# A reordered opening and a mixed gating and pooling stage in a two-branch encoder kernel on eight cores

## The chip, the cores and the metric

The kernel runs on one Trainium2 chip, on all 8 of its cores. Each core works on its own share of the data and no core talks to another. The time of a run is device microseconds of the slowest core. Five engines of a core matter here. PE (TensorE) multiplies matrices and writes to PSUM. DVE (VectorE), ACT (ScalarE) and POOL (GpSimd) do elementwise work. SP (SyncE) issues transfers only. ACT and POOL have DMA queues of their own as well. Each engine executes its own instructions in program order and waits on semaphores for the others.

## What is computed

One layer of a streaming encoder. Each row of x (1024 channels) is normalised and multiplied by `w_in`, which gives seven parts. They feed two branches, whose outputs are merged and projected back:

```python
h = _rmsnorm(x, norm_g)
a, g_a, u, v, g_b, r_a, r_b = jnp.split(h @ w_in, idx, axis=-1)   # 512 x5, 1024 x2
# A: per group of 128 channels, mean over a trailing window of 2/4/8/16 rows, minus a itself
pa = pool_mix(a, prev, pos0)
y_a = (silu(g_a) * (pa @ w_pool[g] * pool_scale)) @ w_a
# B: layer norm of v over its 512 channels, then rows mixed inside chunks of 128 positions
y_b = (silu(g_b) * (u * (W_s @ layernorm(v) + b_s))) @ w_b
y = x + (sigmoid(r_a) * y_a + sigmoid(r_b) * y_b) @ w_o
out = _rmsnorm(y, final_g)
```

There are 4 prompt streams of 8192 rows and 32 sample streams of 64 rows with a 15-row history for the pooling branch. A core gets half a prompt stream (4096 rows), 16 rows ahead of it (the halo, `xh`), and 4 sample streams (256 rows). Last rows of `a` and the normalised `v` of the sample rows are outputs too.

## The kernel before

The rows of a core are cut into eight prompt tiles of 512 rows and one sample tile of 256 rows. The sample tile is second. The first two tiles, t0 (prompt) and t1 (sample), are worked on together, since during them the weights are still arriving. From the third tile on each runs alone.

Weights come as blocks: `Win` is 18 blocks of 256 output columns, named by the part they belong to (C_V, C_GB, C_U, C_A, C_GA, C_RA, C_RB and +256), and `Wa`, `Wb` are four blocks each. All are cast from float32 to bfloat16 on the way, so they go through POOL's queue. `load_weights(n)` issues the next n blocks of a list, `order`. Each issue stands in POOL's program among small arithmetic (line 298 to 300, 1/sqrt of a mean; line 388, the mean of v), so it goes out only when POOL has reached it.

A tile passes these steps:

- x, 128 rows at a time ("sub-tile"): ACT squares and sums (`prep_square`, line 308), POOL makes 1/sqrt, DVE scales (`prep_scale`, line 317). In the opening PE transposes (line 332) and ACT copies the result to `hT` (line 336). Later tiles are transposed by DMA.
- v: PE multiplies (line 352, in the opening by halves of 256 columns, line 373). DVE takes statistics (lines 385 and 386), POOL makes scale and shift, and DVE (line 392) or ACT (line 395) normalises into `n`. For the sample tile ACT does this twice (line 399).
- stage B, four groups of 128 channels: PE makes g_b, ACT takes silu (line 478), PE makes u, DVE multiplies (line 483). One group later PE mixes positions (`z_group`, line 499), DVE adds the bias (line 512) and multiplies into `s` (line 515).
- stage A, four groups: PE makes a and g_a, ACT copies a (lines 430 or 426) and takes silu of g_a (line 434). Window sums are one to four doublings (line 443), on DVE for prompt tiles and on POOL for the sample tile. DVE subtracts (line 450), fixes the first 16 rows (lines 454, 456) and saves the last 16 (line 461). `a_finish` multiplies by `w_pool` on PE (the matmul with `Wp`) and DVE scales into `fa` (line 468).
- stage M, eight blocks: PE makes r_a and r_b, ACT takes sigmoids, PE multiplies `fa` by `Wa` and `s` by `Wb`, DVE merges (lines 531 to 537). Stage O: PE multiplies by `Wo` (line 544), DVE adds x, normalises and SP stores.

The order on every engine is the order in which the code calls these helpers. Nothing is rescheduled. `Sched` turns the named reads and writes of each call into semaphore waits. Three rings of buffers tie the engines to each other: 8 PSUM banks (`next_ps`), 10 work buffers in SBUF (`next_tmp`) and 5 buffers for x. A taker of a ring buffer waits for the last reader of what was there.

The opening is written out by hand (lines 669 to 795). Then stage B runs for t0 and t1 alternately, group by group, then stage A in the same way, then M of t0, M of t1, O of both. Matmuls that only spread a row over partitions (lines 687, 720, 636) come first on PE.

Of the kernel before, what the change touches and what calls it, by code (L numbers as in the profile page):

```python
# [12 lines left out]
P = 128  # L13
# [5 lines left out]
H = 16  # L19
# [105 lines left out]
def build_program(NT):  # L125
# [35 lines left out]
    with ExitStack() as st:  # L161
# [162 lines left out]

        def transpose_pe(xi, dst, kdst, n=P):
            bank, bk = next_ps()
            ptv = bfview(bank)

            def tr(e):
# [90 lines left out]
        def a_group(t, g):  # L420
# [52 lines left out]
        def gb_mm(t, g):  # L473
            return win_group(t, C_GB + g * P)
# [183 lines left out]
        def make_invc():  # L658
# [4 lines left out]
            for g, w in enumerate(WINDOWS):  # L663
# [38 lines left out]

        order = [C_GB, C_U, C_GB + 256, C_U + 256, C_A, C_GA, "Wp", C_A + 256, C_GA + 256]
        for i in range(4):
# [34 lines left out]

        def start_v(i, h=None):  # L740
            if i not in vb:
                vb[i] = next_ps()
            for hh in range(2) if h is None else (h,):
                v_half(*subs[i], hh, *vb[i])

        def start_stats(i):
            return v_stats(*subs[i], *vb[i], i < 4)

        early = {}
        cb = spread_bs()  # L750
        pk = start_square(0)
        xk[2] = load_x_sub(t0, 2, (), "act")
        xk[4] = load_x_sub(t1, 0, (), "act")
        S.add("act", lambda e: e.activation(out=identb[:, :], in_=identf[:, :], func=AF.Copy), ["identf"], ["identb"])
        c = start_xpose(0, prep_scale(pk))
        cb()
        for i in range(1, 4):
            xi = prep_scale(start_square(i))
            c()
# [36 lines left out]

# [34 lines left out]
        def stage_B(ts, pend, early=(), before_z=None):  # L831
# [159 lines left out]
```

How the kernel before makes its waits and increments, by code:

```python
    def emit_engine(self, eng_name, eng):  # L98
        seen = {}
        for op in self.ops[eng_name]:
            for d in op.deps:
                sem, val = d.token
                if seen.get(id(sem), 0) >= val:
                    continue
                seen[id(sem)] = val
                eng.wait_ge(sem, val)
            ins = op.emit(eng)
            if op.token is not None:
                if op.is_dma:
                    ins.then_inc(op.token[0], 16)
                else:
                    ins.then_inc(op.token[0], 1)
```

## Time and profile before

| what | value |
|---|---|
| median of 3 runs | 833.52 us (833.43 to 834.39) |
| the profiled execution's own time | 833.35 us |
| its span, first to last instruction | 831.8 us (cores 829.7 to 831.8) |
| PE busy | 801.5 us (96%) |
| DVE, ACT, POOL busy | 490.8 us (59%), 272.8 us (33%), 119.2 us (14%) |
| mean granted clock of TensorE, by core | 0.992 to 0.997 |
| first x transpose on PE | starts at 10.08 us |
| first matmul of stage B | starts at 42.76 us |
| first matmul with Wa (merging of t0) | starts at 95.84 us |

The page is of the slowest core. PE busy is the time that matmuls cover. They overlap, so the step from one start to the next is shorter than what one lasts. Idle time of PE is shown with what ended it. In the opening the engines wait for x and weights and for each other. From 100 us on PE hardly waits.

### The profile page before, as it was taken

The page shows a single profiled execution, that of the slowest core. Times are in us where ns is not written, and L with a number is a line of the kernel's source. Part 1 is how long each engine was busy: PE and PEld are TensorE (multiplying, and loading weights), DVE is VectorE, ACT ScalarE, POOL GpSimd, SP SyncE. Part 2 cuts the span into 40 slices and gives each one's busy share as a digit, 9 for nine tenths or more (in the row PEclk, how much of TensorE's full clock was granted, in tenths as well). Part 3 has the DMA queues.
Part 4 walks back from the last instruction along what each step waited for, and adds up shares of the span by engine and source line. Part 5 has one row for each costly group of instructions (what it writes and reads, how often), then busy time and mean ns, then how long its engine had stood idle before and what let it go on. Part 6 is the DMA issues. An engine that isn't in the chain of part 4 may idle for free.

```text
span 831.8 us, 13064 instructions; the slowest of 8 cores (829.7 to 831.8 us)
## 1 busy us (share of the span) xinstructions
PE 801.5 (96%) x4032; PEld 389.1 (47%) x4032; DVE 490.8 (59%) x801; ACT 272.8 (33%) x456; POOL 119.2 (14%) x296
## 2 busy tenths in 40 slices
PE   5899899998999999999999999999999999999996
PEld 2665446643444444444444444444444444444442
DVE  3567435676564765458555765567655856466445
ACT  3333223324333424233432423242423433242222
POOL 2461401130001101030002101120102001110001
PEclk9999999999999999999999999999999999999998
DMA  8989782753023411514041603423060502420302
GB/s 206 149 118 172 127 211 45 174 187 96 1 54 99 143 61 26 127 63 141 1 84 69 193 11 39 114 96 108 14 129 37 177 2 39 113 102 1 104 1 102
DMA packets 50950, 77.68 MB, mean 93 GB/s; under 512 B 33385, under 2 KB 33385, under 8 KB 50626
## 3 DMA queue, kind: packets, MB, share of 16 engines
q1 hardware_dynamic: 46030, 62.03, 26.6%
q0 software_dynamic: 4560, 13.76, 10.3%
q10 hardware_dynamic: 292, 1.05, 0.4%
q8 instruction: 34, 0.56, 0.3%
q14 instruction: 34, 0.28, 0.1%
HBM read 64.75 MB, written 18.50 MB: 100 GB/s over the span
## 4 chain that ended last, share of the span: by engine, by line
PE 79%; DVE 10%; issue 5%; DMA 2%; POOL 2%; ACT 1%; DVEq 0%; POOLq 0%; ACTq 0%
PE ps L352 63%; PE ps L544 14%; DVE tmp L443 5%; DMA xr<-xp 2%; PE ps L499 1%; POOL stats L300 1%; DVE pa L450 1%; DVE fa L468 1%; ACT junk L560 1%; PE ps L373 1%; DVE carry L461 1%; DVE xr L556 1%; DVE tmp L431 0%; DVE stats L385 0%; POOL tmp L443 0%
## 5 line engine op out<-in xcount | busy, mean ns | idle before, releaser
L352 PE MATMUL ps<-hT,Win 128*128 128x512 bf16 (+1 forms) x2304 | 492.4, 367 | 1.7 <-DVE n_buf L392 1.0
L352 PEld LDWEIGHTS ps<-hT,Win 128*128 128x128 bf16 x2304 | 224.2, 98 | 239.5 <-issue 3.4
L531 DVE TENSOR_TENSOR tmp<-ps,tmp 128x512 f32<-128x512 f32 (+1 forms) x72 | 47.6, 662 | 141.9 <-PE ps L352 133.4
L298 POOL TENSOR_SCALAR stats<-stats 128x1 f32<-128x1 f32 x103 | 21.1, 205 | 640.8 <-ACT junk L308 313.0
L544 PE MATMUL ps<-Wo,mg 128*128 128x512 bf16 x512 | 111.8, 379 | 0.0
L523 ACT ACTIVATE tmp<-ps 128x512 f32<-128x512 f32 (+1 forms) x72 | 41.3, 574 | 147.7 <-PE ps L352 146.1
L544 PEld LDWEIGHTS ps<-Wo,mg 128*128 128x128 bf16 x512 | 50.1, 98 | 60.1
L556 DVE TENSOR_TENSOR xr<-ps,xr 128x512 f32<-128x512 f32 x68 | 46.8, 689 | 46.4 <-PE ps L544 42.0
L352 PE MATMUL ps<-s_bf,Wb 128*128 128x512 bf16 x256 | 66.6, 383 | 0.0
L352 PE MATMUL ps<-fa,Wa 128*128 128x512 bf16 x256 | 66.0, 380 | 0.4 <-DVE fa L468 0.4
L526 ACT ACTIVATE tmp<-ps 128x512 f32<-128x512 f32 (+1 forms) x72 | 41.3, 573 | 64.6 <-PE ps L352 64.6
L560 ACT ACTIVATE junk<-xr 128x1024 bf16<-128x1024 f32 x34 | 36.0, 1058 | 76.3 <-DVE xr L556 76.3
L443 DVE TENSOR_TENSOR tmp<-tmp 128x512 f32<-128x512 f32 (+3 forms) x80 | 55.8, 697 | 8.3
L300 POOL TENSOR_TENSOR stats<-stats,cols 128x1 f32<-128x1 f32 x103 | 58.2, 565 | 15.5 <-POOL stats L298 1.0
L535 DVE TENSOR_TENSOR tmp<-ps,tmp 128x512 f32<-128x512 f32 (+1 forms) x72 | 47.6, 661 | 12.3 <-PE ps L352 8.1
L317 DVE SCALAR_TENSOR_TENSOR xn<-xr,stats,g_row 128x1024 bf16<-128x1024 f32 x33 | 42.2, 1280 | 15.0 <-POOL stats L300 12.9
L568 DVE SCALAR_TENSOR_TENSOR xr<-xr,stats,fg_row 128x1024 f32<-128x1024 f32 x34 | 43.5, 1278 | 12.6 <-POOL stats L300 12.6
L352 PE MATMUL ps<-Win,hT 128*128 128x512 bf16 x224 | 49.5, 379 | 0.0
L483 DVE TENSOR_TENSOR tmp<-ps,tmp 128x512 f32<-128x512 f32 (+1 forms) x36 | 23.6, 659 | 43.4 <-PE ps L352 39.9
L478 ACT ACTIVATE tmp<-ps 128x512 f32<-128x512 f32 (+1 forms) x36 | 20.5, 574 | 87.2 <-PE ps L352 83.7
L537 DVE TENSOR_TENSOR mg<-tmp 128x512 bf16<-128x512 f32 x64 | 44.3, 692 | 7.7 <-DVE tmp L535 1.6
L395 ACT ACTIVATE n_buf<-ps,stats 128x512 bf16<-128x512 f32 x28 | 21.8, 780 | 57.0 <-POOL stats L388 56.3
(99 smaller groups left out, 516.1 us busy)
## 6 DMA issues: line engine op xcount, KB each, us to landing
xr<-xp SPq DMA_DIRECT2D x63, 512.0 KB, 8.3
yp<-xr SPq DMA_DIRECT2D x32, 512.0 KB, 2.7
Win<-w_in POOLq DMA_DIRECT2D x18, 512.0 KB, 16.8
Wo<-w_o POOLq DMA_DIRECT2D x2, 1024.0 KB, 12.7
Wa<-w_a POOLq DMA_DIRECT2D x4, 256.0 KB, 32.8
Wb<-w_b POOLq DMA_DIRECT2D x4, 256.0 KB, 33.9
xr<-xs SPq DMA_DIRECT2D x2, 512.0 KB, 7.5
ys<-xr SPq DMA_DIRECT2D x2, 512.0 KB, 3.4
```

Source lines behind the costliest of these rows:

```text
L300: S.add("pool", lambda e: e.tensor_tensor(out=rs[0:nparts, :], in0=tt[0:nparts, :], in1=neghalf[0:nparts, :], op=ALU.pow), [ktt, "neghalf" ...
L317: S.add("dve", lambda e: e.scalar_tensor_tensor(out=xn[xi][0:nparts, :], in0=buf[0:nparts, :], scalar=rs[0:nparts, :], in1=g_row[0:nparts, ...
L352: ins = e.matmul(out=bank[:, 0:cols_n], lhsT=l, rhs=r, start=(i == 0), stop=(i == n - 1))
L443: S.add(eng, lambda e, dst=dst, src=src, lo=lo, k=k: e.tensor_tensor(out=tv(dst, lo, L, t.sample), in0=tv(src, lo, L, t.sample), in1=tv(sr ...
L523: S.add("act", lambda e: e.activation(out=sa[:, 0:T], in_=ba[:, 0:T], func=AF.Sigmoid), [ka], [ksa])
L531: S.add("dve", lambda e: e.tensor_tensor(out=sa[:, 0:T], in0=ya[:, 0:T], in1=sa[:, 0:T], op=ALU.mult), [kya, ksa], [ksa])
L535: S.add("dve", lambda e: e.tensor_tensor(out=sbt[:, 0:T], in0=yb[:, 0:T], in1=sbt[:, 0:T], op=ALU.mult), [kyb, ksb], [ksb])
L537: S.add("dve", lambda e: e.tensor_tensor(out=t.mg[:, j, :], in0=sa[:, 0:T], in1=sbt[:, 0:T], op=ALU.add), [ksa, ksb], [t.kmg[j]])
L544: ins = e.matmul(out=bank[:, :], lhsT=t.mg[:, kc, s * P:(s + 1) * P], rhs=Wo[:, h, kc, :], start=(kc == 0), stop=(kc == 7))
L556: S.add("dve", lambda e, h=h, bank=bank: e.tensor_tensor(out=xr[xk][:, h * 512:(h + 1) * 512], in0=bank[:, :], in1=xr[xk][:, h * 512:(h + ...
L560: S.add("act", lambda e: e.activation(out=junk[:, :], in_=xr[xk][:, :], func=AF.Square, accum_out=ss), [("x", xk)], [kss, "junk"])
L568: S.add("dve", lambda e: e.scalar_tensor_tensor(out=xr[xk][:, :], in0=xr[xk][:, :], scalar=rs, in1=fg_row[:, :], op0=ALU.mult, op1=ALU.mul ...
```

## The change

In the opening, before: SP's queue loads x sub-tiles 0, 1 and 3 of t0, then the halo and sub-tile 1 of the sample tile. ACT's queue loads sub-tile 2 of t0 and sub-tile 0 of the sample tile. After: SP's queue loads sub-tiles 0 and 1, the halo, sub-tile 2 of t0 and sub-tile 0 of the sample tile. ACT's loads sub-tile 3 and sub-tile 1 of the sample tile. Steps are called in another order: the halo is squared, scaled and transposed right after sub-tile 1, and the halves of v are grouped. Eleven matmuls of 512 columns on a buffer of ones (`s_bf`, set by a new memset on DVE) are put into PE's program ahead of some steps, with results that nobody reads (`fill`). Of the statistics of v, DVE normalises only sub-tile 0, ACT the rest. The second of two equal computations of `invc` is the one that stays. The weight list has C_A, C_GA and Wp ahead of C_GB+256 and C_U+256, and one more block is issued singly in the opening, with 3 in place of 8 at its end.

Stages B and A of t0 and t1 become one, `stage_AB`, with 16 steps in a fixed sequence. `a_finish` of a prompt group comes two steps after its group. The sample tile's subtraction (`a_mean`, split off `a_group`) comes one step after its group and its `a_finish` one later.

```diff
+        def fill(bank, bk, n):
+            def mm(e):
+                ins = None
+                for _ in range(n):
+                    ins = e.matmul(out=bank[:, :], lhsT=s_bf[:, 0, 0:P], rhs=s_bf[:, 0, :], start=True, stop=True)
+                return ins
+            if n:
+                S.add("pe", mm, [("s", 0)], [bk])
...
+        dma("sp", kx["h"][0][0:H, :], xh_d[:, :], [], ["wo_h"], "c", "loadxh")
+        x0.append(load_x_sub(t0, 2))
+        xs0 = load_x_sub(t1, 0)
...
+        S.add("dve", lambda e: e.memset(s_bf[:, 0, :], 1.0), [], [("s", 0)])
...
-        x0.append(load_x_sub(t0, 3))
-        dma("sp", kx["h"][0][0:H, :], xh_d[:, :], [], ["wo_h"], "c", "loadxh")
-        dma("sp", kx["s1"][0], xs_d[P:2 * P, :], [], ["wo_x"], "c", "loadx")
...
-        order = [C_GB, C_U, C_GB + 256, C_U + 256, C_A, C_GA, "Wp", C_A + 256, C_GA + 256]
+        order = [C_GB, C_U, C_A, C_GA, "Wp", C_GB + 256, C_U + 256, C_A + 256, C_GA + 256]
...
+        sq(0)
+        x0.append(load_x_sub(t0, 3, (), "act"))
+        xk[3] = x0[3]
+        dma("act", kx["s1"][0], xs_d[P:2 * P, :], [], ["wo_x"], "c", "loadx")
...
+        sc(0)
+        tr(0, 2)
         cb()
+        sq(1)
+        sc(1)
+        cp[0]()
+        tr(1, 2)
+        sq("h")
+        sc("h")
+        cp[1]()
+        tr("h")
+        vm(0, 0, nfill=3)
+        cp["h"]()
+        vm(1, 0)
+        sq(2)
+        sc(2)
+        tr(2, 4)
+        sq(3)
+        load_weights(1)
+        sc(3)
+        cp[2]()
+        tr(3)
+        cp[3]()
+        sq(4)
+        load_weights(1)
+        vm(0, 1)
+        vm(1, 1)
+        n0 = vs(0, True)
+        vm(2, 0, 1)
+        sc(4)
+        vm(3, 0, 1)
+        tr(4)
+        sq(5)
+        load_weights(1)
+        n1 = vs(1)
         n0()
+        sc(5)
+        cp[4]()
+        tr(5)
...
+        load_weights(3)
...
+            seq = [("B", tp, 0), ("B", ts, 0), ("B", tp, 1), ("A", tp, 0), ("B", ts, 1), ("A", ts, 0), ("A", tp, 1),
+                   ("B", tp, 2), ("A", ts, 1), ("B", ts, 2), ("A", tp, 3), ("B", tp, 3), ("A", ts, 3), ("B", ts, 3),
+                   ("A", tp, 2), ("A", ts, 2)]
+            zq, aq, mq = [], [], []
+            for i, (kind, t, g) in enumerate(seq):
+                if kind == "A":
+                    if t.first:
+                        carry_in(g)
+                    ag = a_group(t, g)
+                    if t.sample:
+                        mq.append((i + 1, t, ag))
+                    else:
+                        aq.append((i + 2, t, ag()))
+                else:
+                    zq.append((i + 1, t, gb_group(t, g, early)))
+                while aq and aq[0][0] <= i:
+                    a_finish(*aq.pop(0)[1:])
...
-        stage_B([t0, t1], [], early, set_up)
-        pend = stage_A([t0, t1])
+        pend = stage_AB(t0, t1, early, set_up)
```

In the diff `sq`, `sc`, `tr`, `cp`, `vm` and `vs` are square, scale, transpose (with so many fill-ins ahead), copy to `hT`, halves of v, and statistics of v. Their argument is the sub-tile: 0 to 3 of t0, 4 and 5 of the sample tile, "h" the halo.

How the order on the engines changes is shown at three places. First PE's program in the opening before: `identb,xn` are transposes of x, `Win,hT` halves of v (8 per half), 128x512 with `hT,Win` groups of g_b.

```order
L636 MATMUL ps<-Wo,ones 128x512
L332 MATMUL ps<-identb,xn 128x128 x16
L373 MATMUL ps<-Win,hT 128x256 x8
L332 MATMUL ps<-identb,xn 128x128 x8
L373 MATMUL ps<-Win,hT 128x256 x8
L332 MATMUL ps<-identb,xn 128x128 x8
L373 MATMUL ps<-Win,hT 128x256 x32
L332 MATMUL ps<-identb,xn 128x128 x8
L373 MATMUL ps<-Win,hT 128x256 x16
L332 MATMUL ps<-identb,xn 128x128 x8
L352 MATMUL ps<-hT,Win 128x512 x8
L373 MATMUL ps<-Win,hT 128x256 x16
```

And the same place after, where `ps<-s_bf` are the fill-ins:

```order
L650 MATMUL ps<-Wo,ones 128x512
L329 MATMUL ps<-s_bf 128x512 x2
L342 MATMUL ps<-identb,xn 128x128 x8
L329 MATMUL ps<-s_bf 128x512 x2
L342 MATMUL ps<-identb,xn 128x128 x8
L342 MATMUL ps<-identb,xn 128x16 x8
L329 MATMUL ps<-s_bf 128x512 x3
L383 MATMUL ps<-Win,hT 128x256 x16
L329 MATMUL ps<-s_bf 128x512 x4
L342 MATMUL ps<-identb,xn 128x128 x16
L383 MATMUL ps<-Win,hT 128x256 x48
L342 MATMUL ps<-identb,xn 128x128 x16
```

The halo's transpose moved from the end of the opening to a place ahead of the first half of v, both first halves stand ahead of the transpose of sub-tile 2, and 48 matmuls of v (six halves) follow the transpose of sub-tile 3 in one piece. All eleven fill-ins stand ahead of the transpose of sub-tile 2, in fours, threes and twos, as shown.

Second, PE's program where pooling ends and merging begins, before: `pa,Wp` are the matmuls of `a_finish`, 128x512 of t0 and 128x256 of the sample tile.

```order
L352 MATMUL ps<-hT,Win 128x512 x16
L352 MATMUL ps<-pa,Wp 128x256
L352 MATMUL ps<-hT,Win 128x256 x16
L352 MATMUL ps<-hTh,Win 128x16 x8
L352 MATMUL ps<-pa,Wp 128x512
L352 MATMUL ps<-hT,Win 128x512 x16
L352 MATMUL ps<-pa,Wp 128x256
L352 MATMUL ps<-hT,Win 128x256 x16
L352 MATMUL ps<-hT,Win 128x512 x16
L352 MATMUL ps<-pa,Wp 128x512
L352 MATMUL ps<-pa,Wp 128x256
L352 MATMUL ps<-fa,Wa 128x512 x4
```

After:

```order
L513 MATMUL ps<-WTp,n_buf 128x128 x4
L362 MATMUL ps<-hT,Win 128x256 x16
L362 MATMUL ps<-hTh,Win 128x16 x8
L362 MATMUL ps<-hT,Win 128x512 x16
L362 MATMUL ps<-pa,Wp 128x256
L513 MATMUL ps<-WTs,junk 128x128 x2
L362 MATMUL ps<-hT,Win 128x256 x16
L362 MATMUL ps<-hT,Win 128x512 x16
L362 MATMUL ps<-pa,Wp 128x512
L362 MATMUL ps<-pa,Wp 128x256
L362 MATMUL ps<-fa,Wa 128x512 x4
L362 MATMUL ps<-s_bf,Wb 128x512 x4
```

The last pooling group of each tile is now group 2 (three doublings) in place of group 3 (four). A group of B of the sample tile and the two position-mixing steps (line 513) stand between the pooling groups. The r_a and r_b groups (128x512 x16 ahead of the last two `pa,Wp`) keep their place.

Third, DVE's program at the same end, after: line 453 doubles, 464 subtracts, 482 scales into `fa` (written as `hT` for the sample tile), 526 and 529 are the position-mixing step, 497 multiplies by u.

```order
L441 COPY tmp<-carry 128x16
L453 TENSOR_TENSOR tmp<-tmp 128x518
L453 TENSOR_TENSOR tmp<-tmp 128x516
L453 TENSOR_TENSOR tmp<-tmp 128x512
L464 SCALAR_TENSOR_TENSOR pa<-tmp 128x512
L468 TENSOR_TENSOR tmpc<-tmp,invc 128x16
L470 TENSOR_TENSOR pa<-tmpc,tmp 128x16
L475 COPY carry<-tmp 128x16
L482 SCALAR_TENSOR_TENSOR hT<-ps,cols,tmp 128x256
L526 SCALAR_TENSOR_TENSOR tmp<-ps,cols,B 128x256
L529 TENSOR_TENSOR hT<-tmp 128x256
L464 SCALAR_TENSOR_TENSOR pa<-tmp 128x256
```

The scaling of sample group 3 into `fa` (line 482, `hT`) stands behind the whole pooling chain of prompt group 2, and the sample tile's last subtraction (line 464, 128x256) behind the position-mixing step.

## Rows read from the trace of the kernel before

**Rows 1.** Waits of PE, 0 to 140 us: total us, times, longest us.

```profile
PE ps L332 <- DVE xn L317: 9.5, 4, 6.1
PE ps L352 <- DVE carry L461: 2.3, 3, 1.6
...
PE ps L352 <- ACT tmp L478: 0.7, 1, 0.7
```

**Rows 2.** The same view of PE, 97 to 832 us.

```profile
PE ps L352 <- DVE carry L461: 3.8, 8, 1.4
```

**Rows 3.** Busy us in stretches: five engines, granted clock, DMA share, GB/s.

```profile
38.00:42.00 4.00, 4.00 (x31) 2.81 (x30) 3.01 (x5) 0.00 (x0) 1.20 (x4) 1.00 0.32 64
47.00:96.00 49.00, 43.84 (x303) 26.51 (x304) 33.54 (x78) 16.61 (x35) 20.55 (x38) 1.00 1.03 164
96.00:98.00 2.00, 2.00 (x7) 0.80 (x6) 0.75 (x2) 0.00 (x0) 1.79 (x3) 0.60 0.71 124
```

**Rows 4.** Timeline of PE, opening: start us, us, what [idle before <-releaser].

```profile
12.12 1.01 PE L332 MATMUL ps<-identb,xn 128*128 128x128 bf16 x8 [1.03 <-DVE xn L317]
14.22 1.86 PE L373 MATMUL ps<-Win,hT 128*128 128x256 bf16 x8 [1.09 <-DMA Win<-w_in]
22.23 1.01 PE L332 MATMUL ps<-identb,xn 128*128 128x128 bf16 x8 [6.14 <-DVE xn L317]
...
25.60 4.90 PE L373 MATMUL ps<-Win,hT 128*128 128x256 bf16 x32
...
37.16 1.91 PE L373 MATMUL ps<-Win,hT 128*128 128x256 bf16 x16
...
42.76 3.65 PE L352 MATMUL ps<-hT,Win 128*128 128x512 bf16 x24
```

**Rows 5.** Chain of waits, opening: start us, us, what.

```profile
6.06 12.16 DMA xr<-xp
...
20.01 0.56 POOL stats L300
20.80 1.30 DVE xn L317
```

**Rows 6.** Timeline of ACT, opening: a square and a copy of transposed x.

```profile
18.36 1.06 ACT L308 ACTIVATE junk<-xr 128x1024 bf16<-128x1024 f32 x1 [6.15 <-DMA xr<-xp]
...
23.34 1.02 ACT L336 ACTIVATE hT<-ps 128x1024 bf16<-128x1024 bf16 x1 [1.88 <-PE ps L332]
```

**Rows 7.** DMA issues at 2.2, 6.1, 20.5, 22.8 us; last is us to landing.

```profile
xr<-xp SPq DMA_DIRECT2D x1, 512.0 KB, 12.2
...
xr<-xp ACTq DMA_DIRECT2D x1, 512.0 KB, 12.2
...
Win<-w_in POOLq DMA_DIRECT2D x1, 512.0 KB, 12.6
...
Win<-w_in POOLq DMA_DIRECT2D x1, 512.0 KB, 13.7
```

**Rows 8.** The page's groups: normalising v, line 395.

```profile
L395 ACT ACTIVATE n_buf<-ps,stats 128x512 bf16<-128x512 f32 x28 | 21.8, 780 | 57.0 <-POOL stats L388 56.3
```

**Rows 9.** Timeline of PE, pooling groups and start of merging.

```profile
83.52 0.38 PE L352 MATMUL ps<-pa,Wp 128*128 128x512 bf16 x1 [1.59 <-DVE carry L461]
...
95.18 0.27 PE L352 MATMUL ps<-pa,Wp 128*128 128x256 bf16 x1 [2.30 <-DVE pa L450]
95.84 1.35 PE L352 MATMUL ps<-fa,Wa 128*128 128x512 bf16 x4 [0.39 <-DVE fa L468]
...
98.69 4.18 PE L352 MATMUL ps<-hT,Win 128*128 128x512 bf16 x16
...
104.43 3.62 PE L352 MATMUL ps<-hT,Win 128*128 128x512 bf16 x16
```

**Rows 10.** Timeline of DVE, pooling chain of group 2 of the prompt tile.

```profile
79.35 2.30 DVE L443 TENSOR_TENSOR tmp<-tmp 128x518 f32<-128x518 f32 x3
```

**Rows 11.** Timeline of POOL, pooling chain of group 3 of the sample tile.

```profile
92.02 2.37 POOL L443 TENSOR_TENSOR tmp<-tmp 128x304 f32<-128x304 f32 x3 [1.53 <-DVE hT L468]
```

More of the change, by code:

```diff
@@ L323, in bfview, with transpose_pe @@
             return bank[:, :].bitcast(BF16).rearrange("p (k t) -> p k t", k=8)
-        def transpose_pe(xi, dst, kdst, n=P):
+        def fill(bank, bk, n):
[6 more added lines that the diff above has]
+                S.add("pe", mm, [("s", 0)], [bk])
+        def transpose_pe(xi, dst, kdst, n=P, nfill=0):
             bank, bk = next_ps()
             ptv = bfview(bank)
+            fill(bank, bk, nfill)
             def tr(e):
@@ new lines, in build_program, with sq, sc, tr @@
+        vb, pk, xi, cp = {}, {}, {}, {}
+        def sq(i):
+            pk[i] = prep_square("h", H) if i == "h" else prep_square(xk[i])
+        def sc(i):
+            xi[i] = prep_scale(pk[i])
+        def tr(i, nfill=0):
+            if i == "h":
+                cp[i] = transpose_pe(xi[i], hTh[:, :, :], "hTh", H)
+            else:
+                t, s = subs[i]
+                cp[i] = transpose_pe(xi[i], t.hT[:, :, s * P:(s + 1) * P], t.khT[s], P, nfill)
+        def vm(i, *hs, nfill=0):
@@ L741, in start_v, with vs @@
             if i not in vb:
                 vb[i] = next_ps()
[L743 to L747, printed above, removed]
+                fill(*vb[i], nfill)
+            for h in hs:
+                v_half(*subs[i], h, *vb[i])
+        def vs(i, dve=False):
+            return v_stats(*subs[i], *vb[i], dve)
         early = {}
         cb = spread_bs()
-        pk = start_square(0)
@@ new lines, in build_program @@
+        n0()
+        sc(5)
+        cp[4]()
+        tr(5)
+        n2 = vs(2)
+        load_weights(1)
+        cp[5]()
+        n3 = vs(3)
+        load_weights(1)
+        vm(4, 0, 1)
+        n1()
+        eb0 = gb_mm(t0, 0)
+        n2()
+        n3()
+        vm(5, 0, 1)
+        n4 = vs(4)
+        load_weights(1)
+        early[(t0, 0)] = gb_act(t0, *eb0)
+        eb1 = gb_mm(t0, 1)
+        n5 = vs(5)
+        early[(t0, 1)] = gb_act(t0, *eb1)
+        n4()
+        n5()
+        load_weights(3)
@@ L844, in stage_B, with stage_AB @@
                 z_group(*x)
+        def stage_AB(tp, ts, early, before_z):
+            seq = [("B", tp, 0), ("B", ts, 0), ("B", tp, 1), ("A", tp, 0), ("B", ts, 1), ("A", ts, 0), ("A", tp, 1),
[11 more added lines that the diff above has]
+                        aq.append((i + 2, t, ag()))
+                else:
+                    zq.append((i + 1, t, gb_group(t, g, early)))
+                while aq and aq[0][0] <= i:
+                    a_finish(*aq.pop(0)[1:])
+                while zq and zq[0][0] <= i:
+                    if before_z is not None:
+                        before_z()
+                        before_z = None
+                    z_group(*zq.pop(0)[1:])
+                while mq and mq[0][0] <= i:
+                    mi, mt, mean = mq.pop(0)
+                    aq.append((mi + 1, mt, mean()))
+                    aq.sort(key=lambda x: x[0])
+            for _, t, gg in zq:
+                z_group(t, gg)
+            return [x[1:] for x in aq] + [(mt, mean()) for _, mt, mean in mq]
         def stage_M(t, nxt, nx, mid=(), at2=None):
```

52 lines of the change are left out of this document (5 added, 47 removed).

## The prediction

> **What bounds the kernel now.** I read the waits of PE first, in two stretches. From 97 us to the end they are 3.8 us in all [rows 2], with PE busy 96% of the span. Whatever brings merging of t0 forward therefore moves everything behind it, and the end, by as much. Up to 97 us there are long waits: 9.5 us for scaled x, 2.3 us for the pooling chain in three pieces, 0.7 us for a silu [rows 1], and 2.30 and 0.39 us where pooling ends [rows 9]. DVE is busy only 33.5 of the 49 us of stages B and A [rows 3], so those waits are bad order, not too much work. The reader is to see two places: the opening up to 42.76 us, where stage B starts [rows 4], and the stage from there to 95.84 us, where merging starts [rows 9].
>
> In the opening the timeline of PE shows one hole of 6.14 us before the transpose of sub-tile 2 at 22.23 us [rows 4]. The chain of waits puts it down to a transfer issued on ACT's queue at 6.06 us that took 12.16 us [rows 5].
>
> **The opening, step by step.** Sub-tile 2 goes onto SP's queue, where the third large load took 12.2 us from 2.2 us, so it lands near 14.4 us. Sub-tile 3 takes its place on ACT's queue and lands near 18.2 us, after the same 12.2 us [rows 7]. The bytes are the same, so I let the two swap places and no more.
>
> From landing to transpose the trace shows 22.23 - 18.22 = 4.0 us: square on ACT, 1/sqrt on POOL, 1.30 us of scaling on DVE [rows 5, 6]. Before, sub-tile 2's transpose stood there at 22.23 us. After, it is sub-tile 3's. PE's side has to keep up: the halo's square starts behind the first copy on ACT, at about 12.2 us, and with 1.06 us of square, 0.9 of POOL and 1.3 of DVE its transpose comes at about 16 us. Then come 3 fill-ins, two halves of v and 4 fill-ins. In the row at 14.22 us 8 matmuls of 256 columns take 1.86 us, and later 16 take 1.91 us [rows 4]: the first is TensorE at 1.2 GHz, the second at 2.4. A fill-in of 512 columns is thus 0.43 or 0.22 us. At the low clock PE is through at 16 + 0.3 + 1.3 + 3.5 + 1.7 = 22.8 us, and sub-tile 3 is transposed at 24.7 us. At the high clock from the second half of v on it is 21.5 us, and sub-tile 3 goes at 22.7 us. I take 22.7.
>
> The clock itself: before, 32 halves' matmuls from 25.60 us took 4.90 us [rows 4], where the high clock gives about 3.5. So it rose only after some 5 us of unbroken work from 22.23 us on. After, unbroken work begins at 16 us with fill-ins, and the rise should fall at 20 to 21 us.
>
> The Trainium skill, "TensorE: Matmul & The Clock Gate", Part 4, says that transposes do not count as PE being busy for the clock. If so, the fill-ins are what raises it here and the transposes of sub-tiles 2 and 3 are a quiet 1.2 us; the row at 22.23 us begins with a transpose and cannot tell the two apart. By that rule the rise could come later, at the price of the first rival below.
>
> Next, 48 matmuls at 0.109 us are 5.2 us, to 27.9. What is late then is the sample tile's x on ACT: copy of sub-tile 3 after 23.3 us (1.0 us [rows 6]), square 4 at 24.1, scaling behind POOL at 26.4, statistics and normalising of sub-tiles 0 and 1 on DVE (2.3 us), scaling 5 at 29.4, transpose 5 at 30.8. Behind it ACT copies (1.0) and normalises v of sub-tile 1 (0.78 [rows 8]), whose bank the first g_b group takes: 33.3 us. The C_GB weights, issued after sub-tile 3's 1/sqrt at 20.5 us as before, land 12.6 us later, at 33.1 [rows 7]: the same moment. Then g_b, v of sub-tile 5 and g_b, 1.75 us each, end at 38.65. C_U lands no later than 36.5 us (22.8 + 13.7 before [rows 7]). Stage B starts at 38.7 in place of 42.76: **-4.1 us**. Bounds: nothing of this comes before C_GB and 5.25 us of matmuls, and were it 1.4 us earlier in landing I get -5.5; with every step at the low clock -1.7. The new memset on DVE is under 0.5 us and stands ahead of work on DVE that waits for PE's spreading matmuls, so I cost it at nothing; without that cover it costs its 0.5 us.
>
> **Weights.** The DMA engines were only 0.32 busy from 38 to 42 us, and 1.03 from 47 to 96 [rows 3]. A block of w_in takes 3.4 us (36.5 - 33.1 [rows 7]). After, POOL issues C_A near 29 and C_GA near 33 us, so the queue does not run dry: C_U 36.5, C_A 39.9, C_GA 43.2, Wp 44, then C_GB+256 and C_U+256 by 51, C_A+256 and C_GA+256 by 58. The first pooling group stands near 46 us, the group that takes C_U+256 near 57, that with C_A+256 near 64, merging's first blocks near 82 against a landing of 65. No wait, with 3 us of margin at the narrowest.
>
> **The mixed stage.** PE's work is the same. From 42.76 to 95.84 are 53.1 us, of which 0.7 + 2.3 + 2.30 + 0.39 are waits. Now the pooling chain of a prompt group (2.30 us of doublings for group 2 [rows 10], one more 0.8 for group 3, and 1.4 around them) has 3.45 to 5.2 us of other matmuls to hide behind, since `a_finish` comes two steps later. For group 3: 5.0 us of DVE against 6.9 us of PE. I find none late except at the end. There, counted from the end of the first matmul group of prompt group 2: ACT's copy 0.8, DVE's chain 3.9, then scaling of sample group 3 (0.5), for whose work buffer the copy of sample group 2 waits. Then ACT copies (0.6), POOL copies the history and makes three doublings, 2.37 us [rows 11], 0.6 more around them, DVE subtracts (0.5) and scales prompt group 2 (0.75): 10.0 us with semaphores. PE has 1.75 + 0.3 + 1.75 + 3.45 + 0.2 = 7.5 to 7.8 us. So 2.2 us of waits remain, in two pieces. Waits go from 5.7 to 2.2: **-3.5 us**. Bounds: -4.7 (1 us left) and -1 (most waits come back).
>
> After the 2.30 us wait the granted clock is 0.60 of full in the next stretch [rows 3]: 16 matmuls at 98.69 us take 4.18 us, later 3.62 [rows 9]. From 95.84 to 102.70 us that costs 0.3 + 0.85 + 0.6 = about 1.8 us. No such dip followed the 1.59 us wait at 83.52 [rows 9]. The longest remaining wait should be about 1.5 us, so I take the dip as gone: **-1.8 us**, bounds 0 and -1.8.
>
> **Sum.** 833.35 - 4.1 - 3.5 - 1.8 = 824.0 us. The profiled execution's 833.35 us is 0.2 below the median of the runs, 833.52, and its span 831.8 is 1.6 below its own time. I leave the 0.2 out.
>
> **Rivals.**
> 1. The clock stays at 1.2 GHz through the 48 matmuls of v. They take 10.2 us, to about 33.2, transpose 5 ends at 34 and stage B starts at 41.1: 2.4 us later, 826.4. For it: it is low at 14.22 us [rows 4] in spite of the float32 matmuls ahead of it on PE. Against: seven fill-ins and 16 matmuls in one run.
> 2. The waits of the mixed stage move instead of going. For it: with ten work buffers, a silu of a g_b group waits for the scaling of an older pooling group, behind a whole chain on DVE. Then the stage gives 1 us and the dip stays: 833.35 - 4.1 - 1.0 = 828.3. Against: DVE's 33.5 of 49 us in this stage.
> 3. The two queues do nothing. The 16 DMA engines are full, and if the landings set the opening, stage B starts as before: 833.35 - 3.5 - 1.8 = 828.1. For it: C_GB's landing already binds at 33.1 us. Against: what followed that landing before was 9.6 us of further work, of which the change puts half ahead of it.
> 4. Slower: each pooling chain of the prompt tile is exposed in full, because the group behind it takes a work buffer or a bank that the chain still holds. The four chains are 2.0, 2.8, 4.6 and 3.7 us of DVE, 13.1 in all. 833.35 - 4.1 - 5.7 + 13.1 = 836.7. It decides from 9.8 us of new waits on. Against: eight banks span four pairs of groups.
>
> The Trainium skill, "DMA: Bandwidth & Descriptors", section "Issuing engines are not separate DMA queues", says that DMAs issued by different engines run on the same 16 DMA engines and interleave. That is the third rival's rule, and it speaks against any gain in bandwidth from the second queue. The share of 1.03 in the trace agrees with it. My sum uses only the order of landing.
>
> **Chances.** Forecast 0.55 (its own range 821.5 to 826), first rival 0.12, second 0.17, third 0.10, fourth 0.06. To hold the time 8 times in 10 the range goes from 820.5, near the sum of the best bounds (833.35 - 5.5 - 4.7 - 1.8 = 821.4) with a little below, to 828.7, past the second and third rivals. What a measurement of this kernel can tell from no change is about 0.2%, 1.7 us. Only the fourth case is slower: 0.06. The same time needs cases two and three together in part: 0.02. Faster: 0.92.
>
> **What would show it.** The transpose of sub-tile 2 near 20 us and of sub-tile 3 near 22.7. The 48 matmuls in about 5.2 us, not 10.2. The first g_b group at 33.3 us, waiting for ACT's normalising or C_GB. Stage B at 38.7. No wait of PE for weights. Merging at 95.84 - 4.1 - 3.5 = 88.2 us, with one or two waits of 2.2 us in sum ahead of it, for DVE's line 464 and 482, and a granted clock of 1.00 behind them. From there the two traces should run alike. I am wrong if PE waits inside the mixed stage for a silu, if stage B starts after 41 us, or if PE's waits after 90 us grow past 3.8 us.

## The result, and the profile after

| | before | after |
|---|---|---|
| median, same chip | 833.95 us (6 runs, 833.21 to 834.79) | 829.38 us (6 runs; five of them 828.78 to 829.78) |
| ratio | | 0.9946, 95% interval 0.9935 to 0.9956 |
| span of the profiled execution | 831.8 us (core 7) | 828.0 us (core 2; cores 825.7 to 828.0) |
| stage B starts | 42.76 us | 41.65 us |
| first matmul with Wa | 95.84 us | 90.73 us |

The change gains 4.6 us where 9.4 were forecast. 829.4 lies outside the range of 820.5 to 828.7. The direction was right, the size was not. Medians here and below count every execution and ranges the fast ones only; in a slow execution the cores of one die show a lower clock (one of the six above, 912.16 us).

The opening first. This is the timeline of PE on core 2, the slowest (start us, us, engine, line, what it writes and reads, idle before and its releaser). It answers to [rows 4]; `s_bf` on line 329 is a fill-in.

```profile
16.28 0.36 PE L342 MATMUL ps<-identb,xn 16*128 16x16 bf16 x8 [3.28 <-DVE xn L317]
16.57 1.46 PE L329 MATMUL ps<-s_bf 128*128 128x512 bf16 x3
17.82 3.62 PE L383 MATMUL ps<-Win,hT 128*128 128x256 bf16 x16
21.23 1.68 PE L329 MATMUL ps<-s_bf 128*128 128x512 bf16 x4
22.74 1.06 PE L342 MATMUL ps<-identb,xn 128*128 128x128 bf16 x16
23.64 5.40 PE L383 MATMUL ps<-Win,hT 128*128 128x256 bf16 x48
29.01 0.61 PE L342 MATMUL ps<-identb,xn 128*128 128x128 bf16 x8
32.57 0.86 PE L342 MATMUL ps<-identb,xn 128*128 128x128 bf16 x8 [2.95 <-DVE xn L317]
33.22 3.36 PE L383 MATMUL ps<-Win,hT 128*128 128x256 bf16 x16
36.42 1.89 PE L362 MATMUL ps<-hT,Win 128*128 128x512 bf16 x8
38.15 1.91 PE L383 MATMUL ps<-Win,hT 128*128 128x256 bf16 x16
39.90 5.36 PE L362 MATMUL ps<-hT,Win 128*128 128x512 bf16 x32
```

The hole of 6.14 us is gone, and 48 matmuls of v run in 5.40 us. But a hole of 2.95 us has come at 29.6 us, ahead of transpose 5, and 16 matmuls behind it take 3.36 us where as many take 1.91 at 38.15 us. The last row is g_b's second group (8), u of t0 and the sample tile's first group, so stage B starts 1.75 us into it, at 41.65 us.

What transpose 5 waited for stands on ACT, POOL and DVE. ACT, which answers to [rows 6] (two copies of transposed x, then the squares of sub-tiles 4 and 5):

```profile
23.45 1.94 ACT L346 ACTIVATE hT<-ps 128x1024 bf16<-128x1024 bf16 x2 [4.08 <-PE ps L342]
25.27 1.06 ACT L308 ACTIVATE junk<-xr 128x1024 bf16<-128x1024 f32 x1
...
26.52 1.06 ACT L308 ACTIVATE junk<-Wo 128x1024 bf16<-128x1024 f32 x1
```

POOL, the same stretch, from the 1/sqrt of sub-tile 4 on. The steps from 28.12 to 30.07 us belong to the statistics of v of sub-tile 0, which stand ahead of the 1/sqrt of sub-tile 5 (its last step is the row at 30.49):

```profile
26.59 0.18 POOL L298 TENSOR_SCALAR stats<-stats 128x1 f32<-128x1 f32 x1 [4.67 <-ACT junk L308]
26.92 0.56 POOL L300 TENSOR_TENSOR stats<-stats,cols 128x1 f32<-128x1 f32 x1
27.44 0.60 POOL L268 DMA_DIRECT2D Win<-w_in  x1
28.12 0.80 POOL L298 TENSOR_SCALAR stats<-stats 128x1 f32<-128x1 f32 x1
...
30.49 0.55 POOL L300 TENSOR_TENSOR stats<-stats,cols 128x1 f32<-128x1 f32 x1
```

And DVE, the scalings of sub-tiles 4 and 5:

```profile
27.58 1.28 DVE L317 SCALAR_TENSOR_TENSOR xn<-xr,stats,g_row 128x1024 bf16<-128x1024 f32 x1 [1.41 <-POOL stats L300]
...
31.14 1.28 DVE L317 SCALAR_TENSOR_TENSOR xn<-Wo,stats,g_row 128x1024 bf16<-128x1024 f32 x1 [0.15 <-POOL stats L300]
```

Next the waits of PE from 0 to 140 us (total us, times, longest us), to be set against [rows 1]. The pooling waits of 2.3 us in three pieces and the silu's 0.7 have gone:

```profile
PE ps L342 <- DVE xn L317: 6.2, 2, 3.3
PE ps L362 <- DVE pa L464: 1.9, 1, 1.9
```

Where merging starts, PE's timeline after, against [rows 9]:

```profile
87.94 0.38 PE L362 MATMUL ps<-pa,Wp 128*128 128x512 bf16 x1
90.18 0.27 PE L362 MATMUL ps<-pa,Wp 128*128 128x256 bf16 x1 [1.85 <-DVE pa L464]
90.73 1.83 PE L362 MATMUL ps<-fa,Wa 128*128 128x512 bf16 x4 [0.29 <-DVE fa L482]
...
97.59 1.03 PE L362 MATMUL ps<-fa,Wa 128*128 128x512 bf16 x4
```

Four matmuls with `Wa` take 1.83 us at 90.73 and 1.03 us at 97.59. The stretches of [rows 3] after (the columns there) show both low phases, 32 to 36 and 91 to 97 us, in the granted clock (0.60 and 0.73):

```profile
32.00:36.00 4.00, 3.43 (x22) 2.67 (x23) 2.01 (x5) 2.37 (x3) 3.05 (x8) 0.60 1.05 166
91.00:97.00 6.00, 6.00 (x22) 2.40 (x21) 2.18 (x4) 0.60 (x1) 3.80 (x4) 0.73 0.46 81
```

### The profile page after: what moved, and what is told of

It is laid out like the page before. It is cut to its first block, busy times and chain, and to the rows that moved or that the text cites. A ratio compares the mean times of both kernels' runs of the same rounds, so it can differ in the third digit from the quotient of the medians.

```text
span 828.0 us, 13071 instructions; the slowest of 8 cores (825.7 to 828.0 us)
## 1 busy us (share of the span) xinstructions
PE 804.5 (97%) x4043; PEld 389.2 (47%) x4043; DVE 487.4 (59%) x791; ACT 274.8 (33%) x459; POOL 121.2 (15%) x296
## 4 chain that ended last, share of the span: by engine, by line
PE 85%; DVE 7%; issue 4%; ACT 2%; POOL 1%; DMA 0%; DVEq 0%; POOLq 0%; ACTq 0%
PE ps L362 67%; PE ps L558 14%; DVE tmp L453 4%; PE ps L383 1%; PE ps L513 1%; DVE fa L482 1%; ACT junk L574 1%; POOL stats L300 1%; DVE pa L464 0%; PE ps L329 0%; PE ps L735 0%; DVE carry L475 0%; DVE xr L570 0%; DVE tmp L441 0%; DMA mg<-norm_g 0%
## 5 line engine op out<-in xcount | busy, mean ns | idle before, releaser
L298 POOL TENSOR_SCALAR stats<-stats 128x1 f32<-128x1 f32 (+1 forms) x103 | 23.4, 227 | 634.8 <-ACT junk L308 312.9
L453 DVE TENSOR_TENSOR tmp<-tmp 128x512 f32<-128x512 f32 (+4 forms) x80 | 55.8, 697 | 8.3
L300 POOL TENSOR_TENSOR stats<-stats,cols 128x1 f32<-128x1 f32 (+1 forms) x103 | 58.2, 565 | 15.3 <-POOL stats L298 0.2
L492 ACT ACTIVATE tmp<-ps 128x512 f32<-128x512 f32 (+1 forms) x36 | 20.6, 573 | 88.0 <-PE ps L362 80.9
L405 ACT ACTIVATE n_buf<-ps,stats 128x512 bf16<-128x512 f32 x31 | 24.0, 777 | 58.4 <-POOL stats L398 57.8
```

What stands on the lines that cost most here:

```text
L300: S.add("pool", lambda e: e.tensor_tensor(out=rs[0:nparts, :], in0=tt[0:nparts, :], in1=neghalf[0:nparts, :], op=ALU.pow), [ktt, "neghalf" ...
```

## The experiments

Every kernel was timed in five rounds against the kernel before on the same chip. "Edit" is against the changed kernel unless it says otherwise. mixed_only, opening_only, no_fill and early_squares shared a chip (before: 833.22 us). after_again, early_nofill and the two fill_before runs shared another (833.59), and queues_only, ntmp11, early_merge and early_ntmp11 a third (833.53). A difference between two medians of one chip has no interval of its own; where I lean on one, I say whether the two kernels' executions overlap.

### The halves of the change: mixed_only, opening_only

mixed_only is the kernel before with the new stage and weight list; opening_only is the changed kernel with the old stages. This is the edit of opening_only:

```diff
-        pend = stage_AB(t0, t1, early, set_up)
+        stage_B([t0, t1], [], early, set_up)
+        pend = stage_A([t0, t1])
```

> The opening of the kernel before, with the mixed stage of 16 steps and the new order of the weight list. Theory A (the two parts add up, and the mixed stage is worth the 4.0 us that lie between the starts of stage B and merging in the two traces, 53.1 against 49.1 us): about 830.0 us, 4 us under before, stage B starting at 42.8 and merging near 91.8 us. Rival B (the mixed stage needs the weights that the new opening brings earlier): PE waits for C_A or C_GA near 47 us and the gain is 2 us or less, 832 us.

Measured: 830.68 us, ratio 0.9965 [0.9946, 0.9983]. Merging starts at 93.03 us on the slowest core, not near 91.8:

```profile
92.48 0.27 PE L352 MATMUL ps<-pa,Wp 128*128 128x256 bf16 x1 [1.85 <-DVE pa L454]
93.03 1.02 PE L352 MATMUL ps<-fa,Wa 128*128 128x512 bf16 x4 [0.29 <-DVE fa L472]
```

Stage B had started at 41.52 us, so the mixed stage lasts 51.5 us here and 49.08 in the change. Two waits of PE early in the stage, both for ACT, are the difference; in the change only 0.18 us of them are left:

```profile
46.18 1.10 PE L651 MATMUL ps<-mg,ones 128*128 128x512 f32 x2 [1.01 <-ACT tmp L482]
...
49.00 0.38 PE L503 MATMUL ps<-WTp,n_buf 128*128 128x128 bf16 x4 [1.33 <-ACT WTp L646]
```

Neither theory had this: no wait is for weights, and yet the stage is worth 1.6 us of PE time behind the old opening (53.08 to 51.5) and 4.0 behind the new one. The rest of the 2.5 us may be the clock, which fell in merging on 2 of its 8 cores and on all 8 before.

> The changed kernel with stages B and A apart again, as before, and all of the new opening. Theory A (adds up): stage B starts at 41.7 us, merging near 94.7, and with a last transfer that ends 0.9 us later after the last DVE instruction, as in the trace after, the time is 833.2 to 833.7 us, hardly less than before. Rival B (the opening is worth more than its 1.1 us, and the mixed stage hides it): 831.5 us or less.

Measured: 830.39 us, ratio 0.9961 [0.9944, 0.9978], against the 833.2 to 833.7 expected: that theory fell. I had judged the opening by the slowest core of the profiled run, on which the clock fell. The halves give 2.5 and 2.8 us alone and 4.6 together. The difference of some 0.8 us can't be told from nothing by the intervals, but the end of the program has the same size: it lasts 21.7 to 21.8 us with either half and 22.6 with both (last section).

### Landing order alone: queues_only

The kernel before, with x on the queues as after and nothing else moved:

```diff
+        x0.append(load_x_sub(t0, 2))
+        xs0 = load_x_sub(t1, 0)
...
-        xk[2] = load_x_sub(t0, 2, (), "act")
-        xk[4] = load_x_sub(t1, 0, (), "act")
+        xk[3] = load_x_sub(t0, 3, (), "act")
```

> The kernel before, with the x loads alone put on the queues as in the change: halo, sub-tile 2 of t0 and sub-tile 0 of the sample tile on SP's, sub-tile 3 and the other sample sub-tile on ACT's. Theory A (the order of landing sets the transposes): transpose 2 near 20 us, transpose 3 near 22.3 us in place of 24.7, the halves of v 2 us earlier, stage B 1 to 2 us earlier, 832.0 us. Rival B (the transfers are full anyway, and C_GB's landing at 33 us sets what follows): no change, 833.4 us.

Measured: 831.68 us, ratio 0.9980 [0.9971, 0.9990], 1.85 us faster. On core 2 transpose 2 stands at 20.48 us (22.23 before) behind a wait of 6.07 us (6.14 before), and stage B at 40.88:

```profile
20.48 1.01 PE L332 MATMUL ps<-identb,xn 128*128 128x128 bf16 x8 [6.07 <-DVE xn L317]
...
40.88 3.65 PE L352 MATMUL ps<-hT,Win 128*128 128x512 bf16 x24
```

The third rival is refuted: which x lands first moves transpose 2 by 1.75 us and stage B by 1.88.

### What makes transpose 5 late: early_squares

Square 4 moves ahead of the copies of sub-tiles 2 and 3 on ACT. Square 5 moves up too, so that on POOL its 1/sqrt comes ahead of the statistics of v. The weight issues behind the squares and the scalings on DVE move with them. The run doesn't separate these parts.

```diff
+        sq(4)
+        load_weights(1)
         cp[2]()
         tr(3)
+        sc(4)
         cp[3]()
-        sq(4)
+        sq(5)
         load_weights(1)
...
         vm(2, 0, 1)
-        sc(4)
         vm(3, 0, 1)
         tr(4)
-        sq(5)
-        load_weights(1)
+        sc(5)
         n1 = vs(1)
         n0()
-        sc(5)
```

> The changed kernel with the squares of sub-tiles 4 and 5 ahead of the copies of 2 and 3 on ACT, and their scaling ahead of the statistics on DVE where the buffers allow. Theory A (the opening ends late because ACT copies 2 and 3 first, then squares 4 and 5, with DVE and POOL behind them): square 4 near 21.8 us, transpose 5 near 29.6 us in place of 32.6, no low clock after it, the first g_b group at 33.1 us in place of 36.4, stage B at 38.4 us in place of 41.7, 826.1 us. Rival B (transfers set the end of the opening): the first g_b group is held by C_GB past 35 us and the gain is below 1 us, 828.5 us or more.

Measured: 824.71 us, ratio 0.9886 [0.9853, 0.9920]. PE on core 5:

```profile
22.77 5.40 PE L383 MATMUL ps<-Win,hT 128*128 128x256 bf16 x48
28.01 1.06 PE L342 MATMUL ps<-identb,xn 128*128 128x128 bf16 x16
29.99 1.91 PE L383 MATMUL ps<-Win,hT 128*128 128x256 bf16 x16 [0.93 <-ACT hT L346]
33.17 1.89 PE L362 MATMUL ps<-hT,Win 128*128 128x512 bf16 x8 [1.27 <-ACT n_buf L405]
...
36.64 5.36 PE L362 MATMUL ps<-hT,Win 128*128 128x512 bf16 x32
```

Transposes 4 and 5 now run as one, the 16 halves take 1.91 us and the first g_b group stands at 33.17 us, where the prediction had put it. Stage B is at 38.4. Square 4 starts at 20.30 us instead of 25.27. The result is 1.4 us below the figure that I had expected; 0.6 of it is in the program's last stretch (last section). So the 3 us missing in the opening are the late squares and 1/sqrts of the sample tile and the clock behind their wait.

### What the fill-ins do: no_fill, early_nofill

```diff
-        tr(0, 2)
+        tr(0)
...
-        tr(1, 2)
+        tr(1)
...
-        vm(0, 0, nfill=3)
+        vm(0, 0)
...
-        tr(2, 4)
+        tr(2)
```

> The changed kernel without its eleven fill-in matmuls. Theory A (the fill-ins raise the clock near 22 us, but what they save is taken back by the wait of 2.95 us for the scaled rows of sub-tile 5): the six halves of v take some 7 to 8 us in place of 5.4, the wait shrinks to about 1 us, transpose 5 still comes near 32.6 us, and the time is 829.4 us within 0.5; if the shorter wait also keeps the clock up after it, up to 1.5 us less. Rival B (the clock is on the path): 831.5 us or more.

Measured: 828.05 us, ratio 0.9930 [0.9901, 0.9959]. PE on core 0:

```profile
20.09 1.01 PE L342 MATMUL ps<-identb,xn 128*128 128x128 bf16 x8 [0.60 <-DVE xn L317]
...
23.59 7.59 PE L383 MATMUL ps<-Win,hT 128*128 128x256 bf16 x48
...
32.11 0.61 PE L342 MATMUL ps<-identb,xn 128*128 128x128 bf16 x8 [0.49 <-DVE xn L317]
...
34.66 1.89 PE L362 MATMUL ps<-hT,Win 128*128 128x512 bf16 x8
```

Without fill-ins the 48 matmuls take 7.59 us instead of 5.40. Nothing is lost: transpose 5 comes at 32.11 us all the same, since it hangs on DVE. In the changed kernel PE had merely reached it early and waited, the clock fell in that wait, and g_b came at 36.42 us. Without fill-ins it is at 34.66. On seven of the 8 cores of this run the wait ahead of transpose 5 is 0.2 to 1.7 us and the clock holds; on core 7 it is 2.62 us and the clock falls (0.73 from 32 to 36 us).

With both edits, the expectation and the result:

> Early squares as in the last study, without the eleven fill-ins. Theory A (fill-ins save time on PE only; they were worthless as long as transpose 5 came late, and now PE is what is late): the six halves end near 31 us in place of 28.2, the first g_b group starts near 34 us in place of 33.2, 825.5 us, 0.8 more than with them. Rival B (the fill-ins cost by themselves, as their removal from the changed kernel gained 1.3 us): 823.5 us.

Measured: 827.86 us, ratio 0.9929 [0.9917, 0.9942], 3.2 us slower than early_squares, which ran on another chip (before: 833.59 and 833.22). Theory A had 0.8. On core 3 the 48 matmuls take 7.84 us and g_b stands at 35.55 us, 2.4 later than in early_squares. So the fill-ins are worth some 2 to 3 us once x is early. While it is late they are worth nothing that can be told: the ratios of no_fill and of the change have overlapping intervals.

### The two low phases: fill_before_tr5, fill_before_merge

Twelve fill-ins ahead of transpose 5; or eight ahead of the last `Wp` matmul of the sample tile.

```diff
-        tr(5)
+        tr(5, 12)
```

```diff
             for x in mid:
-                a_finish(*x)
+                a_finish(*x, 8 if x[0].sample else 0)
```

With them ran the changed kernel itself, after_again.

> The changed kernel once more, beside the next three on one chip: 829.4 us within 0.7. Of its trace two things are asked: whether the time from the last DVE instruction's start to the end of the span is again 5.3 us (4.3 before), and on how many cores the clock is low behind the wait for transpose 5 (five of eight in the first trace, slowest core among them).

Measured: 829.29 us, ratio 0.9952 [0.9940, 0.9965].

> The changed kernel with 12 more fill-ins ahead of transpose 5, 2.6 us at the high clock, where PE waits 2.95 us. Theory A (the wait makes the clock fall, and the 16 matmuls of v behind it take 3.36 us in place of 1.75): transpose 5 comes when it came, no core is low at 32 to 36 us, stage B starts at 40.0 us in place of 41.7 on the slowest core, 827.9 us. Rival B (the clock's fall there costs nothing, since the first g_b group waits for ACT's normalising or C_GB): no change, 829.4 us.

Measured: 827.82 us, ratio 0.9933 [0.9920, 0.9945]. Its executions (827.4 to 828.0) and those of after_again (828.3 to 829.8) don't overlap. On the slowest core:

```profile
29.25 2.54 PE L329 MATMUL ps<-s_bf 128*128 128x512 bf16 x11
...
32.26 1.91 PE L383 MATMUL ps<-Win,hT 128*128 128x256 bf16 x16
34.35 1.89 PE L362 MATMUL ps<-hT,Win 128*128 128x512 bf16 x8 [0.19 <-ACT n_buf L405]
```

One of the twelve is missing in the trace. The transpose comes no earlier than DVE lets it, but none of 8 cores has a low clock from 32 to 36 us, and g_b is 2.1 us earlier than on core 2 after.

> The changed kernel with 8 fill-ins, 1.7 us, ahead of the last matmul with Wp, where PE waits 1.85 us before merging. Theory A (that wait makes the clock fall in the first 7 us of merging, 6.86 us from Wa to Wa in place of about 5.2): no core is low at 90 to 97 us, 827.7 us. Rival B (the clock falls for the waits of the opening or by chance, not for this one): as many cores low, 829.4 us or up to 0.3 more for the fill-ins.

Measured: 827.55 us, ratio 0.9929 [0.9917, 0.9942], executions of 827.3 to 827.8. None of 8 cores falls in merging. (Lines are one higher in this kernel.)

```profile
87.52 1.89 PE L329 MATMUL ps<-s_bf 128*128 128x512 bf16 x8
89.44 0.27 PE L363 MATMUL ps<-pa,Wp 128*128 128x256 bf16 x1
90.10 1.02 PE L363 MATMUL ps<-fa,Wa 128*128 128x512 bf16 x4 [0.39 <-DVE fa L483]
...
91.82 3.62 PE L363 MATMUL ps<-hT,Win 128*128 128x512 bf16 x16
```

Filling the waits gives back 1.5 and 1.7 us, though what PE waited for comes no earlier: that is what each low phase costs.

### Where the wait of 1.85 us comes from: ntmp11

On ACT the copy of sample group 2 takes a work buffer. In the changed kernel it waited 2.68 us for DVE's scaling of an older group (line 482), behind a pooling chain; POOL's doublings and the last subtraction follow it:

```profile
86.06 0.38 ACT L436 ACTIVATE tmp<-ps 128x256 f32<-128x256 f32 x1 [2.68 <-DVE hT L482]
```

One buffer more is to free it; its room comes from a small one that moves into memory idle at that time.

```diff
-NTMP = 10
+NTMP = 11
...
-        tmpc = sb("tmpc", [P, H], F32)
...
+        tmpc = mgf[:, 1024:1040]
```

> The changed kernel with 11 work buffers in place of 10 (and the 16-column scratch of the first rows moved into another buffer to make room). Theory A (the wait before merging is the tie between ACT's copy of sample group 2 and DVE's scaling of sample group 3, which hold the same work buffer): the copy comes near 84 us in place of 86, the wait for line 464 goes, 0.9 us of wait for line 482 stays, and no core's clock falls in merging, 826.3 us. Rival B (POOL's doublings and DVE's chain are late by themselves): the wait keeps more than 1.5 us, 829 us.

Measured: 825.92 us, ratio 0.9904 [0.9888, 0.9920]. ACT and PE on core 5:

```profile
83.53 0.38 ACT L436 ACTIVATE tmp<-ps 128x256 f32<-128x256 f32 x1 [0.72 <-PE ps L362]
```

```profile
88.20 0.27 PE L362 MATMUL ps<-pa,Wp 128*128 128x256 bf16 x1 [0.45 <-DVE pa L464]
88.83 1.02 PE L362 MATMUL ps<-fa,Wa 128*128 128x512 bf16 x4 [0.36 <-DVE fa L482]
...
90.55 3.62 PE L362 MATMUL ps<-hT,Win 128*128 128x512 bf16 x16
```

The wait shrinks from 1.85 to 0.45 us and the clock stays up on all 8 cores: 1.4 and about 1.7 us. The median is 3.4 us below after_again's on another chip, where the kernel before differed by 0.06, and the two ratios' intervals are apart.

### Together: early_merge, early_ntmp11

early_squares with the eight fill-ins ahead of merging, and early_squares with the eleventh buffer.

> Early squares together with the 8 fill-ins before merging. Theory A (the two are independent): no low clock in merging on any core, 824.7 - 1.7 = 823.0 us. Rival B (with the earlier opening the slowest core is one that was not low in merging): 824.5 us.

Measured: 824.08 us, ratio 0.9884 [0.9870, 0.9897]. No core falls in merging, but against early_squares (0.9886) that is nothing one can tell. The same fill-ins gave 1.7 us beside the late opening. In early_squares the clock fell in merging on 5 of 8 cores of the profiled run, so I can't say why less comes of it in the medians. The two profiled executions do differ by 1.4 us of span (823.5 and 822.1). Two chips and intervals of 0.7% and 0.3% don't settle it.

> Early squares with 11 work buffers and no fill-ins before merging. Theory A: the wait of 1.9 us shrinks to about 0.9 and the clock stays up, 824.7 - 1.3 - 1.7 = 821.7 us. Rival B (POOL and DVE late by themselves): 824.5 us.

Measured: 822.03 us, ratio 0.9860 [0.9846, 0.9874]. This is the fastest kernel, 7.3 us below after_again. Merging starts at 85.52 us. PE on core 4:

```profile
85.52 1.02 PE L362 MATMUL ps<-fa,Wa 128*128 128x512 bf16 x4 [0.36 <-DVE fa L482]
```

## Why the prediction was wrong, step by step

The spans differ by 3.8 us. The forecast for the same difference was 9.4.

1. **Transposes 2 and 3.** Forecast near 20 and 22.7 us. Both ran at 22.74. The 20 went against my own working, which had PE busy until 21.5 us with what stands ahead of transpose 2. Sub-tile 2 landed at 16.0 us, not 14.4, which delayed nothing: its scaling ended at 20.6. The order of landing worked as said (queues_only: 20.48), but the four fill-ins and both halves of v, at the low clock, held PE until 22.74. No_fill has transpose 2 at 20.09.
2. **48 matmuls in 5.2 us.** Right: 5.40. The first rival (clock low throughout, 10.2 us) is refuted. Even without fill-ins it is 7.59. They ended at 29.0 us, not 27.9, since I had left out the 0.9 us of transposes ahead of them; it cost nothing, as transpose 5 was not ready.
3. **Opening, -4.1 us: this is the step that failed.** It was -1.1 (42.76 to 41.65). The failing clause is "copy of sub-tile 3 after 23.3 us (1.0 us [rows 6]), square 4 at 24.1, scaling behind POOL at 26.4, [...] scaling 5 at 29.4, transpose 5 at 30.8". ACT had two copies to make there, 1.94 us, because PE delivered both transposes together, so square 4 began at 25.27. Scaling 4 began at 27.58. For the next step I had counted DVE's work, but POOL was what came last. From 26.59 to 31.04 us it ran almost without a gap: the 1/sqrt of sub-tile 4, a weight DMA (0.60 us), the statistics of v of sub-tile 0 (whose first step took 0.80 us instead of 0.18), and only then the 1/sqrt of sub-tile 5. Scaling 5 began at 31.14 and transpose 5 at 32.57: 1.8 us late. The 2.95 us wait this left let the clock fall for another 1.5 us. I had costed the lateness of x but not the clock behind it, though my own sum had PE idle from 27.9 to 30.8 us but for one transpose. On cores 1, 4 and 7, where the clock held, stage B starts at 39.5 to 39.7 us; the slowest core is one where it fell. early_squares (stage B at 38.4) shows that the 38.7 was there to be had.
4. **First g_b group at 33.3 us.** 36.42. C_GB landed at 33.0 as forecast, but wasn't what it waited for. In fill_before_merge, whose slowest core kept its clock in the opening, it was: PE waited 1.74 us for `Win`, until 35.77 us. So the landing isn't the same in every execution.
5. **Weights, no wait.** Right: none after the opening in the list of waits.
6. **Mixed stage, -3.5 us.** Right in size: from stage B to merging 53.08 us before and 49.08 after, -4.0. But 2.4 us of it need the new opening (mixed_only), which the working doesn't have. The wait left is 1.85 + 0.29 us against 2.2 forecast. Its origin was named in the working (the copy of sample group 2 waits for a work buffer), and ntmp11 confirms it. The second rival's mechanism was there too: a silu on ACT waited 3.62 us for a buffer, until 75.74 us, at no cost to PE.
7. **The dip in merging, -1.8 us: failed.** I took two pieces of at most 1.5 us, which would not let the clock fall. The wait came in one piece of 1.85 us. From the first Wa to the next is 6.86 us in both traces (95.84 to 102.70, and 90.73 to 97.59). Fill_before_merge and ntmp11 give 1.7 us and a full clock.
8. **Merging at 88.2.** 90.73.
9. **"From there the two traces should run alike": failed by about 1 us.** From the first Wo matmul of the last tile to the end of the span are 21.7 us before (810.10 to 831.8) and 22.6 after (805.37 to 828.0).

-1.1 - 4.0 + 0.4 (from merging to that Wo matmul, 714.26 before on core 7 and 714.64 after on core 2) + 0.9 = -3.8 us. Of the 5.6 us missing, 3.0 are the opening, 1.8 the dip and 1.3 the last two terms, against 0.5 better in the mixed stage. The fourth rival (slower) had no sign of itself: of the 13.1 us of DVE chains all but about 2 were covered.

The range failed with the steps. The opening's -1.1 us lies outside its own bounds of -1.7 to -5.5, since these left out a clock that falls a second time; the dip's 0 was within its bounds. The worst bounds together, 833.35 - 1.7 - 1 = 830.65 us, lay above the range that I gave. I let my likeliest value stand on both being good, though one cause, a wait just before, decides each.

## What to carry to other kernels

Where PE waits before dense work, price the wait twice: its own length, and the low clock that may follow it (here about 1.5 to 1.7 us each). Fill-in matmuls remove the second price but not the first, and pay ahead of time only if PE is what comes last afterwards. When work is regrouped on one engine, walk the feeding engine's program again copy by copy: two transposes delivered together are two copies ahead of the next square. And a part of a change that is worth 4.0 us in the whole can be worth 1.6 by itself: time the parts alone as well.

## What the hardware showed that I had not expected

**Small steps on POOL last as long as DVE's scaling beside them.** The 128x1 step on line 298 takes 0.18 or 0.19 us alone. Begun during a scaling of 1.28 us on DVE it ended with it: at 28.12 + 0.80 = 28.92 against DVE's 27.58 + 1.28 = 28.86, and in the same way in these rows of POOL and DVE:

```profile
19.52 1.14 POOL L298 TENSOR_SCALAR stats<-stats 128x1 f32<-128x1 f32 x1 [0.44 <-ACT junk L308]
```

```profile
19.33 1.28 DVE L317 SCALAR_TENSOR_TENSOR xn<-xr,stats,g_row 128x1024 bf16<-128x1024 f32 x1 [3.19 <-POOL stats L300]
```

20.66 against 20.61. The Trainium skill, "SBUF — State Buffer", section "SBUF: two separate sides", says that VectorE and GpSimd share one pair of ports as an exclusive lock for a whole instruction. These rows agree. Beside DVE's normalising on line 402 (30.18 to 30.99 us), which reads its tensor from PSUM, POOL's step at 30.49 took its usual 0.55 us. I did not take the overlap away in a run of its own.

**The clock falls on some cores only.** After, it is low from 32 to 36 us on cores 0, 2, 3, 5 and 6, and not on 1, 4 and 7, all with the same program. The wait doesn't decide it: ahead of transpose 5 it is 2.62 us on cores 0 and 5, where the clock fell, and on the three where it did not. In after_again it fell on two of 8, all with a wait of 2.62 us. In merging, behind the 1.85 us, it fell on 8 of 8 in the profiled run after, 5 of 8 in after_again, 2 of 8 in mixed_only; behind 0.45 + 0.36 us or fill-ins on none of 32 cores in four kernels. The slowest core sets the time, so one core of 8 is enough to pay. The Trainium skill, "TensorE: Matmul & The Clock Gate", section "What's actually happening", says that the gate's window runs freely and doesn't start with the kernel; that equal programs fare differently agrees with it.

**The end of the program has a length of its own.** From the first Wo matmul of the last tile to the end of the span are 21.7 to 21.8 us in before, mixed_only, opening_only and queues_only, 22.0 to 22.1 in the four kernels with early squares, and 22.6 to 22.7 in the changed kernel (after, after_again) and in the four that differ from it only in fill-ins or work buffers (slowest core of each). In the last group the end of the span comes 5.2 to 5.3 us behind the start of DVE's last instruction, in all the others 4.3 to 4.5. None of them alters that code. The cause is open.
